# Mixing stage on half-array tiles, rotary half-swap by transfers, spatial and pooling products moved among the input slabs

## What is computed

```
proj = rms_norm(x) @ w_in                     # 1024 -> 2816 columns
za, xb, q, k, v, g = split(proj)              # 512, 256, 512, 512, 512, 512 columns
ya = u * (w_masked @ rms_norm(v') + bs)       # u, v' = split(gelu(za)); 4 heads of 64, blocks of 128 tokens
yb = (pooled(xb) - xb) @ b_w * b_scale        # 4 groups of 64, windows 2, 4, 8, 16
q, k = rotary(q) / 8, rotary(k)               # 8 heads of 64: x1*cos - x2*sin, x2*cos + x1*sin
yc = silu(g) * head_norm(retention(q, k, v))  # per head: (q k^T * decay) v, chunk-causal
x = x + concat(ya, yb, yc) @ w_out
x = x + conv_ffn(rms_norm(x))
```

## Time and profile before

| | us |
|---|---|
| median of 3 runs (2013.73 to 2018.99) | 2016.19 |
| profiled execution, device time | 2020.71 |
| its span in the profile | 2018.9 |
| PE busy | 1927.8 |
| DVE busy | 1269.4 |
| ACT busy | 743.1 |

### The profile page before, as it was taken

One profiled execution on the slowest core, in us unless ns is written; L12 is line 12 of the kernel. 1 busy time (PEld: TensorE's weight loads), 2 busy tenths in 40 slices (PEclk: granted clock), 3 DMA queues, 4 the chain that ended last, 5 costly groups with the idle time before them and its releaser, 6 DMA issues.

```text
span 2018.9 us, 24187 instructions
## 1 busy us (share of the span) xinstructions
PE 1927.8 (95%) x8760; PEld 1548.5 (77%) x8760; DVE 1269.4 (63%) x1918; ACT 743.1 (37%) x1010; POOL 216.0 (11%) x51
## 2 busy tenths in 40 slices
PE   7998999999998999999999998999899979999996
PEld 6885778888886886688888886778766748888885
DVE  5435768786877354678877778644476364554565
ACT  5233334233334323243333334344476432322321
POOL 0000000000000000000000000133300214344340
PEclk9998999999999999999999998897699979999998
DMA  6220233333332221033333332321200112222221
GB/s 242 84 84 21 81 107 107 143 111 139 121 128 84 84 84 42 24 123 126 125 125 127 126 132 99 127 83 53 74 1 1 63 42 84 104 101 86 104 95 51
DMA packets 27708, 188.46 MB, mean 93 GB/s; under 512 B 3072, under 2 KB 3456, under 8 KB 5888
## 3 DMA queue, kind: packets, MB, share of 16 engines
q1 hardware_dynamic: 22752, 156.77, 21.8%
q10 hardware_dynamic: 4896, 30.87, 4.3%
HBM read 185.53 MB, written 2.10 MB: 93 GB/s over the span
## 4 chain that ended last, share of the span: by engine, by line
PE 89%; DVE 5%; issue 2%; DMA 2%; ACT 2%; DVEq 0%; SPq 0%; ACTq 0%; PEldq 0%
PE ps L452 26%; PE ps L454 26%; PE ps L453 26%; PE ps L612 2%; PE ps L622 2%; DMA raw<-in_weights 1%; PE ps L844 1%; PE ps L797 1%; PE ps L578 1%; DVE wl L1478 1%; DVE std L1413 1%; DMA x<-in_xin 1%; PE ps L811 1%; PE ps L509 0%; PE ps L501 0%
## 5 line engine op out<-in xcount | busy, mean ns | idle before, releaser
L452 PE MATMUL ps<-xh,wh 128*128 128x512 f32 x1504 | 596.8, 397 | 22.4 <-DVE xl L1440 9.7
L453 PE MATMUL ps<-xl,wh 128*128 128x512 f32 x1504 | 588.6, 391 | 0.0
L454 PE MATMUL ps<-xh,wl 128*128 128x512 f32 x1504 | 588.4, 391 | 0.0
L918 ACT ACTIVATE wh<-raw 128x2048 fp32r<-128x2048 f32 x144 | 275.6, 1914 | 469.4 <-DMA raw<-in_weights 468.4
L435 POOL TENSOR_TENSOR wl<-raw,wh 128x2048 fp32r<-128x2048 f32 x46 | 214.0, 4652 | 1760.4 <-ACT wh L918 1760.4
L452 PEld LDWEIGHTS ps<-xh,wh 128*128 128x128 f32 x1504 | 284.3, 189 | 87.8 <-issue 27.2
L453 PEld LDWEIGHTS ps<-xl,wh 128*128 128x128 f32 x1504 | 284.4, 189 | 61.1 <-issue 3.1
L454 PEld LDWEIGHTS ps<-xh,wl 128*128 128x128 f32 x1504 | 284.2, 189 | 59.9
L1478 DVE TENSOR_TENSOR wl<-raw,wh 128x2048 fp32r<-128x2048 f32 x98 | 224.0, 2285 | 104.9 <-ACT wh L918 104.9
L452 PE MATMUL ps<-ah,wh 128*128 128x512 f32 x608 | 239.2, 393 | 6.2 <-DVE x L1711 3.3
L454 PE MATMUL ps<-ah,wl 128*128 128x512 f32 x608 | 237.7, 391 | 0.0
(11 more groups left out here) (285 smaller groups left out, 2251.8 us busy)
## 6 DMA issues: line engine op xcount, KB each, us to landing
raw<-in_weights SPq DMA_DIRECT2D x144, 1024.0 KB, 4.8
adab<-in_ada ACTq DMA_DIRECT2D x22, 1024.0 KB, 4.7
t<-in_cst ACTq DMA_DIRECT2D x1, 3264.0 KB, 10.8
adab_tail<-in_ada ACTq DMA_DIRECT2D x2, 1024.0 KB, 8.8
out_y<-x SPq DMA_DIRECT2D x8, 256.0 KB, 2.0
raw<-in_weights SPq DMA_DIRECT2D x2, 512.0 KB, 6.8
x<-in_xin SPq DMA_DIRECT2D x2, 512.0 KB, 7.2
x<-in_xin SPq DMA_DIRECT2D x1, 1024.0 KB, 10.8
```

What stands on the lines that cost most here:

```text
L452: pe.matmul(out, w_hi, m_hi, start=start, stop=False)
L453: pe.matmul(out, w_hi, m_lo, start=False, stop=False)
L454: return pe.matmul(out, w_lo, m_hi, start=False, stop=stop)
L918: act.activation(wh[:, s, :], raw[:, s, :], ACT.Copy).then_inc(hi_made, 1)
```

## The change

Seven things are edited, all in the first block, and both layers get them.

1. Input slabs go through three bank pairs (c % 3, banks 0 to 5), and PE waits for slab c - 3. `sum_added` moves from behind slab 0 to behind slab 1, the turn of `rstd` from behind slab 1 to behind slab 2. ACT and DVE split slab 3 ahead of root and reciprocal.
2. `rot` and its 8 products per layer go. ACT issues four transfers for q (behind the split of slab 7) and four for k (behind that of slab 9) that copy 32 partitions each from SBUF to SBUF into `turned`, with the halves of the heads swapped; the sign is in the sin table. DVE's `rope` is three operations of 128 x 2048 for q and three for k.
3. Spatial products run behind slab 5, 16 of 128 columns into half-array tiles (64 output rows each) in banks 6 and 7. DVE's `ya` is two operations of 128 rows in place of four of 64, right behind `rope` of q.
4. Pooling products run behind slab 7, also with 64 output rows; ACT copies two full banks.
5. Retention goes by pairs of heads. Scores: each product takes the 64 rows of its head (rows 0 to 63 or 64 to 127), side by side, into two banks. Values: each gives 64 output rows, side by side, into one bank. `kpad`, `vcur`, `stage_pair`, `bw_cur`, the zeroing on POOL and the loop go. DVE multiplies two heads in one operation.
6. The head norm takes squares and roots on ACT with eps as bias; DVE has 4 reciprocals as before, one per tile, placed tile by tile.
7. Output slabs use bank pairs 0, 4, 2, 6; slabs 11 and 12 take features 4 to 7 one tile at a time; slab 13 waits for the fourth root, not for the addition to x.

```diff
                 for c in range(W_IN):
-                    if c >= 2:
-                        evacuated(c - 2)
+                    if c >= 3:
+                        evacuated(c - 3)
...
-                    if c == 0:
+                    if c == 1:
...
                         sum_added(l * 2, l * 2, sqb)
...
+                    if c == 5:
...
+                        for j in range(2):
+                            for i in range(NT):
+                                for hh in range(2):
+                                    a = (l * 4 + 2 * j + hh) * P
+                                    last = pe.matmul(ps[HD * hh:HD * hh + HD, 6 + j, i * P:(i + 1) * P],
+                                                     va[:, i, j * P + HD * hh:j * P + HD * hh + HD], ws_f[:, a:a + P],
+                                                     start=True, stop=True)
...
-                        for i in range(4):
-                            if o:
-                                pe.wait_ge(rope_part, l * 8 + i + 1)
-                            pe.matmul(bank(4 + i), rot, src[:, i, :], start=True, stop=True).then_inc(rot_ready, 1)
...
+                        for pair in range(2):
+                            pe.wait_ge(ya_part, l * 2 + pair + 1)
+                            for hh in range(2):
+                                g = 2 * pair + hh
+                                h = slice(HD * hh, HD * hh + HD)
+                                for j in range(NT):
+                                    pe.matmul(ps[h, 6 + pair, j * P:(j + 1) * P], xb[:, j, g * HD:(g + 1) * HD],
+                                              band[:, min(j, 1), g, 0:P], start=(j == 0), stop=False)
...
+                def ret_scores(p):
+                    for n, unit in enumerate(s_units):
+                        if p:
+                            pe.wait_ge(sT_ready, l * 12 + 3 * (p - 1) + n + 1)
+                        for j in unit:
+                            w = S - j * P
+                            for hh in range(2):
+                                h = slice(HD * hh, HD * hh + HD)
+                                last = pe.matmul(ps[:, s_banks[j][hh], s_cols[j]:s_cols[j] + w], k[h, p, j * P:(j + 1) * P],
+                                                 q[h, p, j * P:S], start=True, stop=True)
...
+                def ret_values(p):
+                    pe.wait_ge(sT_ready, l * 12 + 3 * p + 3)
...
+                    for j in (0, 1, 3, 2):
+                        w = S - j * P
+                        for hh in range(2):
+                            h = slice(HD * hh, HD * hh + HD)
+                            last = pe.matmul(ps[h, 2, j * P:S], vr[:, j, p * P + HD * hh:p * P + HD * hh + HD],
+                                             sT[:, p % 2, hh, soffs[j]:soffs[j] + w], start=(j == 0), stop=(j == 2))
...
+                def turn_halves(t):
+
+                    for b in range(4):
+                        o = b ^ 1
+                        act.dma_start(turned[32 * b:32 * b + 32, :, :], t[32 * o:32 * o + 32, :, :]).then_inc(half_turned, 16)
...
+                def rope(t, n):
+
+                    dve.wait_ge(half_turned, (l * 2 + n + 1) * 64)
+                    dve.tensor_tensor(turned[:, :, :], turned[:, :, :], over_tiles(sin), ALU.mult).then_inc(rope_part, 1)
+                    dve.tensor_tensor(t[:, :, :], t[:, :, :], over_tiles(cos), ALU.mult).then_inc(rope_part, 1)
+                    dve.wait_ge(rope_part, (l * 2 + n + 1) * 2)
+                    dve.tensor_tensor(t[:, :, :], t[:, :, :], turned[:, :, :], ALU.add).then_inc(rope_done, 1)
```

More of the change, by code:

```diff
@@ L111, in constants @@
     put(c1, C1, "cos", np.cos(ang))
-    put(c1, C1, "sin", np.sin(ang))
+    put(c1, C1, "sin", np.where(p[:, None] % HD < half, -np.sin(ang), np.sin(ang)))
     lg = np.log1p(-np.exp2(-5.0 - np.arange(RET_HEADS)))
@@ L202, in build @@
         xb = keep("xb", [P, NT, GRP])
+        turned = keep("turned", [P, 4, S])
+        keep("gap", [P, 1024])
         pooled = keep("pooled", [P, 2, S])
-        rtmp = keep("rtmp", [P, 2, S])
-        sT = at("sT", [P, 2, 1280], F32, st_at)
-        gsq = at("gsq", [P, 2, S], F32, st_at)
+        sT = at("sT", [P, 2, 2, 1280], F32, st_at)
+        assert st_at + size([P, 2, 2, 1280]) == top[0]
         q_at = top[0]
@@ L658, in _ @@
-                for w in range(2):
-                    slab_fm(n0 + W_IN + w, (W_IN + w) % RING, bank0[w], fresh=(mix_split, l * 8 + 6), half=half_done,
-                            kts=turned[2:], start=False)
+                    if c == 5:
+                        pe.wait_ge(rt_ready, l + 1)
+                        pe.wait_ge(va_ready, l + 1)
+                        pe.wait_ge(ws_masked, 1)
+                        for j in range(2):
[5 more added lines that the diff above has]
+                                                     start=True, stop=True)
+                            last.then_inc(sv_ready, 1)
@@ L661, in _ @@
+                ret_variance(2)
+                ret_variance(3)
+                slab_fm(n0 + W_IN + 1, (W_IN + 1) % RING, mix_bank[1], kts=others, stop=False)
+                for p in range(4):
+                    for w in range(2):
+                        slab_fm(n0 + W_IN + w, (W_IN + w) % RING, mix_bank[w], fresh=(mix_split, l * 8 + 4 + p),
+                                half=half_done if p == 3 else None, kts=(4 + p,), start=False, stop=p == 3)
                 for w in range(2, W_OUT):
[L662 removed]
@@ new lines, in _ @@
+                evacuate_tokens(1)
+                act.wait_ge(tm_evac, l * 4 + 1)
+                for i in range(NT):
+                    last = act.activation(ya[:, i // 2, (i % 2) * GRP:(i % 2 + 1) * GRP], va[:, i, :], ACT.Square, accum_out=vss[:, 0, i:i + 1])
+                last.then_inc(vss_ready, 1)
+                act.wait_ge(vss_ready, l + 1)
+                act.activation(vss[:, 1, :], vss[:, 0, :], ACT.Sqrt, bias=eps[:, :], scale=1.0 / GRP).then_inc(vstd_ready, 1)
+                for c in range(2, W_IN):
+                    used(n0 + c)
+                    if c in (2, 7, 8):
+                        evacuate_tokens(c)
@@ L1071, in ada_load @@
+                centred_square(1)
+                keep_values(3)
+                deviation(0)
+                centred_square(2)
+                deviation(1)
+                centred_square(3)
+                high_gated(0)
+                deviation(2)
+                deviation(3)
+                ahead(W_IN - 1, n0, n3)
+                for p in range(1, 4):
+                    high_gated(p)
                 def ada_load(a):
@@ L1632, in add_mixed @@
+                low_gated(3)
+                ahead(10)
                 def add_mixed(i):
```

444 lines of the change are left out of this document (186 added, 258 removed).

## The result

| | before | after |
|---|---|---|
| device time, median (range) | 2015.87 us (2013.73 to 2018.99, 4 runs) | **1934.03 us** (1932.1 to 1934.88, 4 runs) |
| ratio after/before, 95% interval | | 0.9592 [0.9575, 0.9608] |
| profiled execution, its span | 2018.9 | 1930.3 |

(The median of before has a fourth run here and is 2015.87.) The page of the changed kernel answers to the earlier trace rows: engines, then the chain of work that ended last.

A forecast was written before the change was run, and what follows sets the result against it. PE, busy 95% of the span, was taken as the bound. Terms -10.8 - 14.4 + 17.2 - 63.0 + 4.8 = -66.2 us took the profiled 2020.7 to 1954.5, for the median 1950 us; range 1935 to 1982.

The forecast's parts named there:

- Between slab 10 and the output slabs: PE's stretch with `bw` products, means, variances, scores and values: 62.9 us falls to 31.4 per layer, -63.0 for both.
- first copy-out and semaphores: Term of the stretch between slab 10 and the output slabs: 1.1 us per layer.
- Changes of form: Thirteen changes between full and half array in the retention stretch: 0.15 us each, 2.0 in all, upper end 0.4 each.
- Spatial and pooling: These products, moved among the input slabs, take 8.6 us per layer there: +17.2; their old time counted elsewhere.
- Rotary: Rotary products of q and k go: four times 3.6 us of PE, -14.4; replacing transfers taken as hidden.
- 19 us: Time left for q's four transfers to land, between issue and the pooling products, after DVE's `rope` and first `ya`.
- Start of a layer: `sum_added` behind slab 1 saves 3.2 us of waiting per layer and half clock after it: -6.0 and -4.8, -10.8.
- Output slabs: Behind slab 11's start, PE waits 1.8 us for tile 6's low part, plus 0.6 for clock and latencies: +4.8 both layers.
- full overlap: Rival, half-array products: second half not held back by first half's second instruction; 1939.5 us, chance 0.25.
- No overlap: Rival, half-array products: they don't overlap, 34.1 us stands for 21.4, spatial is 3.5; 1977 us, chance 0.20.
- late transfers: Rival, q and k copies between partitions: land after 51 us, PE waits 60 us per layer; 2070 us, chance 0.03.
- clock rival: Rival, retention stage: falls to half clock though PE has work, +52, 2002 us; chance 0.04.

The follow-up runs named there:

- one-half experiment: Changed kernel with both heads of a pair on the same half of the array, in scores and values: 1968.53 us.
- two orderings: Changed kernel with a pair's values reordered: all four products of one head, then the other's, 1947.54 us; in groups of two per head, 1934.08 us.
- products by twos: Changed kernel with the values of a pair in groups of two products per head: 1934.08 us.
- the experiment that moves them: Changed kernel with spatial and pooling products, DVE's `ya` and ACT's copies of `pooled` back behind slab 10: 1935.83 us.
- The experiment that undoes it: Changed kernel with the sum of squares (`sum_added`) back behind slab 0, the third bank pair kept: 1946.53 us.

## Why the prediction was off

The forecast was 1950, the range ended at 1935, the median is 1934. Sign, the bound (PE), and the list of what goes were right. The table has 22.4 us that were not forecast. By the steps of the prediction:

- **Between slab 10 and the output slabs, -63.0 forecast, -73.9 measured.** This is where the step that failed lies, in the words "So the second half's first instruction can start no earlier than the first half's second one", which gave 2.67 us per pair and 21.4 per layer. In the records both halves' first instructions start 6 ns apart (154.111 and 154.117 on the recorder's clock, the first scores), and all that follow in pairs 6 or 7 ns apart. A set is 2.13 us of columns and 0.2 for the change of form, so that the columns of all eight are 17.1 us and not 21.4: 4.3 us per layer. A second term of the same sum, 1.1 us per layer for "first copy-out and semaphores", had no row behind it, and the runs show nothing in its place: the first scores start 0.32 us after the last product of slab 10, without a wait. (The old stretch had been read as 62.9 us; the rows give 62.7.) The premise "Starts keep program order in every row of the timeline" was true of every row there: all of them used the whole array, where nothing could be overtaken. It was not evidence on halves. The one-half experiment prices the overlap at 34.4 us, the two orderings show what it asks of the program: the other half's instruction behind at most three of this half's that are still waiting. The Trainium skill, TensorE: Matmul & The Clock Gate, section The mechanism, gives about 4 ns between starts on different tiles; the trace has 6 to 7, and 13 in the products by twos. That section's rule of strict order does not hold in these records, where an instruction starts ahead of three earlier ones.
- **Changes of form**: 0.15 us each as taken; 0.1 to 0.2 are in the rows (sets of scores 0.2 over their columns, a mean 0.1 to 0.2), none of the retention at 0.4.
- **Spatial and pooling, +17.2**: 6.7 us per layer by the experiment that moves them, +13.4 in all, where 8.6 per layer had been taken. Start to start they are 1.90 and 4.38 us against 2.7 and 5.5; the remaining 0.4 is what was taken for changes of form. Spatial overlaps fully (1.7 was the lower bound). Pooling was taken serially, and that was right but for the seams between two heads, where the look-ahead saves some 0.25 us each. The narrow products took about 0.12 us each, two instructions of 0.06, at the lower end of the 0.1 to 0.2 and not the 0.17 of the sum. That the copy of slab 6 or later splits turn up as waits did not happen.
- **Rotary, -14.4**: -13.4 by the same experiment (6.7 per layer). The 3.6 us per tensor were the duration of a row, which runs past the start of the next instruction; eight instructions 0.43 us apart are 3.4. The four transfers of q are issued over 3.1 us and land in 4.2 each, about the 4.7 us of the nearest row and not the far 12.7, and the "19 us" left for them is of the right size: one turn of ACT later costs nothing, two turns 8 us of waiting.
- **Start of a layer, -10.8**: 6.3 in layer 0 and about 5.3 in layer 1, 11.6; the other 1.1 us of the table's first row are the start of the clock. The experiment that undoes it gives 12.4 in the same stretches. Wait plus half clock is the right mechanism. The forecast's 1.6 us of clock in layer 1 are 2.1 by the stretch and 3.0 in the experiment.
- **Output slabs, +4.8**: right place, right operation, wrong size. PE asked for the third tile 18.5 us behind the start of slab 11, as forecast (18.4), but its low part was ready at 19.3 and not at 20.1, since the chain of reciprocals started 0.4 us before slab 11 and not with it. The wait is 0.74 and not 1.8 us, without a loss of clock behind it, +1.0 per layer in all.
- **The rest**: 2.4 us are the FFN wait of one execution. The 1.6 us behind layer 1 lie where nothing was changed and are no more than what executions of one code differ by there; their cause stays open.

Of the rivals, full overlap happened, and it had been given 0.25 against 0.48. Its time, 1939.5, was the better one, and still 5 us high, mostly by the output slabs and the 1.1 us per layer for the copy-out. The range had been cut to it "with one or two waits less", while two further sizes could fall below their middle too. No overlap and late transfers were both brought about in experiments and gave 1968 and, with 8 us of waiting per layer, a loss of 20 us in the two stretches (24 by the medians): their mechanisms are real, their conditions weren't met. The clock rival is out, since the granted clock was 1.00 for all of the retention. Its row had also been read too strongly: PE was busy for the whole of 1387 to 1415 us, but with products of 24 columns as well as of 68; the row's own 10.10 us are those that read `kkh`.

## What to carry to other kernels

Two products that use half the array each cost here as much as one (and 0.2 us per change of form) if at most three instructions for one half stand ahead of the other half's in the program; write the head loop innermost, and look for loops (pooling here) where it is not. A wait of 3 us on a bound TensorE cost 5 to 6 here, since the clock fell behind it, so moving one sum behind more work was worth nearly as much as removing all rotary products (11.6 and 13.4 us). When a trace has no row for a mechanism, order seen where nothing could overlap is no ground for a number: keep the forecast's weight on both bounds.

## What the hardware showed that was not expected

- fp32 products, two instructions each, overlap across halves: 2.36 us for a pair's scores against 4.51 on one half.
- Starts go past a busy half by three instructions, and no version shows more: with three of the first head's between, both heads start 13 ns apart; with seven between, the second starts when the fifth of the first does.
- A product of 128 rows, 16 columns and 64 weights takes about 0.06 us per instruction, where 0.1 was seen with 128 weights.
- Four copies of 256 KB between partitions of SBUF land in 4.2 us each, the last some 7 us after the first was issued; a slab of 1 MB of weights takes 4.8.
- The clock can fall or stay, for the same waits near the end of layer 0 (0.83 and 1.00 over 10 us), in two executions of nearly the same program, and the time changes by only 0.2 us. What decides stays open.
